# Expert rounds: the bias added by TensorE in every chunk, and the transposes of gathered rows placed behind the activation's

## The reference

```python
def expert_block(args):
    x_i, e = args                                # rows of one expert's tokens
    gu = x_i @ w_gate_up[e] + b_gate_up[e]       # 1024 x 2048, and the bias
    gate, up = jnp.split(gu, 2, axis=-1)
    gate = jnp.minimum(gate, SWIGLU_LIMIT)
    up = jnp.clip(up, -SWIGLU_LIMIT, SWIGLU_LIMIT)
    act = (up + 1.0) * (gate * jax.nn.sigmoid(SWIGLU_ALPHA * gate))
    return act @ w_down[e] + b_down[e]           # 1024 x 1024
```

## Time and profile before

| | us |
|---|---|
| median of 3 runs | 2780.39 (2773.59 to 2784.25) |
| the profiled execution | 2776.94 |
| its span | 2775.3 |
| TensorE busy (PE) | 2586.3, 93% |
| TensorE loading weights (PEld) | 2093.9, 75% |
| VectorE (DVE) | 1993.8, 72% |
| ScalarE (ACT) | 1633.8, 59% |
| GpSimd (POOL) | 401.8, 14% |

### The profile page before, as it was taken

How to read it: one execution, slowest core, us unless ns; L and a number is a source line. 1 busy time by engine, 2 the same in 40 slices (tenths; PEclk the granted TensorE clock), 3 DMA queues, 4 the chain that set the end, 5 groups by cost and what they waited for, 6 DMA issues and landing times.

```text
span 2775.3 us, 41771 instructions
## 1 busy us (share of the span) xinstructions
PE 2586.3 (93%) x12297; PEld 2093.9 (75%) x12297; DVE 1993.8 (72%) x2832; ACT 1633.8 (59%) x2352; POOL 401.8 (14%) x518
## 2 busy tenths in 40 slices
PE   4999899996798948999999999999999999999998
PEld 3888667775687737777777888888888888888886
DVE  5333044453655677676767999999999999999998
ACT  5122144343342326565656888888888888888885
POOL 0000010101000231111111211111111112111110
PEclk7999999997799969999999999999999999999999
DMA  6652222211344347767666999999999999999997
GB/s 235 250 193 103 71 88 79 86 50 49 108 139 159 128 162 280 248 236 252 237 232 237 392 372 378 381 378 376 372 378 377 374 376 385 375 371 375 380 377 270
DMA packets 156570, 715.45 MB, mean 258 GB/s; under 512 B 23180, under 2 KB 43582, under 8 KB 91860
## 3 DMA queue, kind: packets, MB, share of 16 engines
q1 hardware_dynamic: 129680, 641.61, 60.0%
q0 software_dynamic: 26752, 72.92, 9.8%
q10 hardware_dynamic: 68, 0.02, 0.0%
HBM read 659.48 MB, written 64.60 MB: 261 GB/s over the span
## 4 chain that ended last, share of the span: by engine, by line
PE 58%; issue 2%; DVE 2%; ACT 1%; ACTq 0%; DVEq 0%
PE e_pgu L90 11%; PE e_pgu L89 11%; PE e_pgu L88 11%; PE e_pdn L88 6%; PE e_pdn L90 5%; PE e_pdn L89 5%; PE e_pat L2411 2%; PE e_pxt L2403 2%; PE e_pgu L2473 1%; PE e_pgu L2416 1%; PE e_pgu L2417 1%; PE e_pdn L2417 1%; PE e_pdn L2416 1%; ACT e_gu_hi L2090 1%; DVE e_act L2725 0%
## 5 line engine op out<-in xcount | busy, mean ns | idle before, releaser
L2094 DVE TENSOR_TENSOR e_gu_lo<-gu_raw,e_gu_hi 128x1024 fp32r<-128x1024 f32 x676 | 800.6, 1219 | 71.2 <-ACT e_gu_hi L2090 65.8
L2090 ACT ACTIVATE e_gu_hi<-gu_raw 128x1024 fp32r<-128x1024 f32 x676 | 681.4, 1055 | 14.0 <-PE e_pgu L90 11.2
L88 PE MATMUL e_pgu<-e_gu_hi,e_x_hi 128*128 128x512 f32 x1344 | 547.0, 407 | 7.1 <-issue 7.1
L90 PE MATMUL e_pgu<-e_gu_hi,e_x_lo 128*128 128x512 f32 x1344 | 528.0, 393 | 0.0
L89 PE MATMUL e_pgu<-e_gu_lo,e_x_hi 128*128 128x512 f32 x1344 | 526.6, 392 | 0.0
L2699 DVE TENSOR_TENSOR e_dn_lo<-dn_raw,e_dn_hi 128x1024 fp32r<-128x1024 f32 x336 | 398.3, 1220 | 9.7 <-ACT e_dn_hi L2516 9.0
L2516 ACT ACTIVATE e_dn_hi<-dn_raw 128x1024 fp32r<-128x1024 f32 x336 | 345.1, 1059 | 5.2 <-PE e_pdn L2417 2.8
L90 PEld LDWEIGHTS e_pgu<-e_gu_hi,e_x_lo 128*128 128x128 f32 x1344 | 252.9, 188 | 54.6
L88 PEld LDWEIGHTS e_pgu<-e_gu_hi,e_x_hi 128*128 128x128 f32 x1344 | 254.0, 189 | 46.3 <-issue 7.5
L89 PEld LDWEIGHTS e_pgu<-e_gu_lo,e_x_hi 128*128 128x128 f32 x1344 | 254.0, 189 | 39.7
L88 PE MATMUL e_pdn<-e_dn_hi,e_a_hi 128*128 128x512 f32 x672 | 266.5, 397 | 5.9 <-DVE e_a_lo L2742 5.9
(11 more groups left out here) (480 smaller groups left out, 4501.5 us busy)
## 6 DMA issues: line engine op xcount, KB each, us to landing
gu_raw<-in_w_gate_up_dram SPq DMA_DIRECT2D x336, 1024.0 KB
dn_raw<-in_w_down_dram SPq DMA_DIRECT2D x168, 1024.0 KB
wada_later<-in_w_ada_dram SPq DMA_DIRECT2D x32, 512.0 KB, 3.7
win_raw<-in_w_in_dram POOLq DMA_DIRECT2D x5, 2048.0 KB
proj_by_token<-out_stage SPq DMA_DIRECT2D x32, 256.0 KB, 2.0
wg_raw<-in_w_in_dram POOLq DMA_DIRECT2D x16, 512.0 KB, 4.5
gates_transposed<-g_stage POOLq DMA_DIRECT2D x32, 256.0 KB
gate_in<-gates_transposed SPq DMA_DIRECT2D x16, 512.0 KB
```

The source lines that it names most:

```text
L88: pe.matmul(out, a[0], w[0], start=first, stop=False)
L90: return pe.matmul(out, a[1], w[0], start=False, stop=last)
L2090: act.activation(m.gu_hi[:, b, 2 * j:2 * j + 2], m.gu_raw[:, b, 2 * j:2 * j + 2].rearrange("p k g n -> p k (g n)"), ACT.Copy).then_inc(m.g ...
L2094: dve.tensor_tensor(m.gu_lo[:, b, 2 * j:2 * j + 2], m.gu_raw[:, b, 2 * j:2 * j + 2].rearrange("p k g n -> p k (g n)"), m.gu_hi[:, b, 2 * j ...
```

## The change

- TensorE adds the bias in every unit: `by_pe` is gone, and with it `with_biases` on VectorE, the branch of `swish` that reads its result, the loads of bias rows with SyncE's wait ahead of them, and the store of bias rows in the routing phase. The rows of final_g, which shared that buffer, get one of their own and no wait. The clamp of `up` is always made from PSUM, behind the wait for `swish`.
- The transposes of gathered rows stand directly behind `turn_a`. In rounds of two: group 0 in (2, slot 1), 1 in (2, slot 0), 2 in (3, slot 1), 3 in (3, slot 0). In rounds of one: group 2 in chunk 2, group 3 in chunk 3. Only a first round of one keeps two groups behind the down product.
- On ScalarE the general list (rounds of two) moves `stage_x` with them, behind `high_a`. In `single` only the arguments of `swish` change.
- At the end of a round of two's last unit, `swish` comes before the second `high_x`, and `activate` before the second `low_x`.

```diff
@@ TensorE, in the loop over k
                         if k == (TURN_A_K if l else 3) and (l or not first):
                             turn_a(n - 1)
-                        if k == FIRST_K and s == 0 and c >= 2 and ahead:
-                            turn_x(r + 1, 2 * c - 3)
+                            if c >= 2 and (s == 0 or two):
+                                turn_x(r + 1, 2 * c - (4 if s else 3) if ahead else c)
...
-                        if k == KT // 2 and by_pe(two, c, s):
+                        if k == KT // 2:
...
-                            if (c, s) == (CH - 1, 1 if two else 0):
+                            if (c, s) == (CH - 1, 0):
                                 ins.then_inc(pick_used, 1)
...
@@ TensorE, behind the down product
-                    if s == 0 and c in (1, 2):
-                        turn_x(r + 1, 2 * c - 2 if ahead else c + 1)
+                    if first and not two and c in (1, 2):
+                        turn_x(r + 1, 2 * c - 2)
@@ ScalarE, swish
-            def swish(n, parity, on_pe, s=0):
+            def swish(n, parity, s=0):
...
-                elif on_pe:
+                else:
                     act.wait_ge(hidden, n + 3)
                     act.wait_ge(activated, n + 1)
                     act.activation(sg[:], p_gu[:, parity, 0], ACT.Gelu_apprx_sigmoid).then_inc(swished, 1)
-                else:
-                    act.wait_ge(with_bias, n + 3)
-                    act.activation(sg[:], gb[:, 0], ACT.Gelu_apprx_sigmoid).then_inc(swished, 1)
@@ ScalarE, rounds of one: stage_x stays where it is
                     if c:
-                        swish(n - 1, (c - 1) % 2, True)
+                        swish(n - 1, (c - 1) % 2)
@@ ScalarE, rounds of two
                         high_a(n - 1, ps if l else 0)
+                    if s == 1 and c >= 2:
+                        if c == 2:
+
+                            act.wait_ge(x1_lo_done, r + 1)
+                        stage_x(r + 1, 2 * c - 4)
                     if s == 0 and c >= 2:
                         stage_x(r + 1, 2 * c - 3)
...
-                        act.wait_ge(hidden, n + 3)
+                        swish(n, l % 2)
                         high_x(r + 1, 1)
-                        swish(n, l % 2, by_pe(two, c, s))
...
-                    if s == 0 and c in (1, 2):
+                    if not two and c in (1, 2):
@@ SyncE
-                    if two and c < CH - 1:
-
-                        wait_apart(sp, with_bias, U + 2 * c + 2)
-                        bs(here, c + 1, (c + 1) % 2)
@@ VectorE
-                    elif l and not by_pe(two, pc, ps):
-                        with_biases(n - 1, pc, (l - 1) % 2, r)
```

More of the change, by code:

```diff
@@ L43 @@
 FC = FF // CH
-FIRST_K = 6
 TURN_A_K = 5
@@ L1928, in _ @@
                 load_dn(m, sp, 0, c, c, m.dn_in[c])
[L1929 to L1932, removed]
         @block.gpsimd
@@ L2107, in phase_experts @@
     with ExitStack() as ctx:
-        gu_raw, dn_raw, bias, pick = m.gu_raw, m.dn_raw, m.gu_bias, m.pick
+        gu_raw, dn_raw, pick = m.gu_raw, m.dn_raw, m.pick
         gu_hi, gu_lo = m.gu_hi, m.gu_lo
@@ L2132, in phase_experts @@
         gu_in, dn_in, gathered, rows_in = m.gu_in, m.dn_in, m.gathered, m.rows_in
-        bias_in = [sem(f"e_bias_in{i}") for i in range(2)]
         gu_hi_done, gu_lo_done = m.gu_hi_done, m.gu_lo_done
@@ L2197, in units @@
                 yield l, c, s, s == 0, seq[l - 1]
-        def by_pe(two, c, s):
-            return not two or c == 0 or s == 1
         def kept(eng, value):
@@ L2612, in single @@
                 act.wait_ge(hidden, swish_last + 3)
-                swish(swish_last, (CH - 1) % 2, True)
+                swish(swish_last, (CH - 1) % 2)
                 high_x(r + 1, 1)
@@ L2650, in body @@
                     if l:
-                        swish(n - 1, (l - 1) % 2, by_pe(two, pc, ps), ps)
+                        swish(n - 1, (l - 1) % 2, ps)
                         if ps:
@@ L2699, in dn_piece @@
                 dve.tensor_tensor(dn_lo[:, b, j], dn_raw[:, b, j], dn_hi[:, b, j].bitcast(F32), ALU.subtract).then_inc(dn_lo_done, 1)
[L2701 to L2706, removed]
             def with_low(n, parity):
@@ L2720, in activate @@
                     return
-                if on_pe:
-                    dve.tensor_scalar(gb[:, 1], p_gu[:, parity, 1], 1.0 - LIMIT, 1.0 + LIMIT, ALU.max, ALU.min).then_inc(up_clamped, 1)
-                    dve.sem_inc(with_bias, 1)
+                dve.tensor_scalar(gb[:, 1], p_gu[:, parity, 1], 1.0 - LIMIT, 1.0 + LIMIT, ALU.max, ALU.min).then_inc(up_clamped, 1)
+                dve.sem_inc(with_bias, 1)
                 dve.wait_ge(up_clamped, n + 3)
@@ L2793, in body @@
                         with_low(n - 1, (l - 1) % 2)
-                    elif l and not by_pe(two, pc, ps):
-                        with_biases(n - 1, pc, (l - 1) % 2, r)
                     piece()
                     if l:
-                        activate(n - 1, (l - 1) % 2, by_pe(two, pc, ps), ps)
+                        activate(n - 1, (l - 1) % 2, ps)
                         piece()
@@ L2805, in body @@
                         low_x(r + 1, 0)
-                        if not by_pe(two, c, s):
-                            with_biases(n, c, l % 2, r)
+                        activate(n, l % 2)
                         low_x(r + 1, 1)
-                        activate(n, l % 2, by_pe(two, c, s))
                     while todo:
@@ L2838, in combine_tiles @@
     k.bd = over("c_bias_rows", [3 * NE, D], F32, dn0)[:]
-    k.gf = over("c_final_g", [P, D], F32, m.gu_bias_at)[:]
+    k.gf = m.final_g_rows[:]
     k.bd3 = over("c_bias_parts", [3 * NE, D], F32R, dn0 + 4 * D)[:]
```

25 lines of the change are left out of this document (4 added, 21 removed).

## The result

The changed kernel is slower: 2928.76 us (median of 5 runs, 2908.14 to 2937.55) against 2778.59 us (5 runs), a ratio of 1.0539 with a 95% interval of 1.0505 to 1.0573. The forecast was 2892 us with a range of 2866 to 2927: right in its sign and in the place and the mechanism of the waits, 37 us too low at the median and 2 us outside the range.

A forecast was written before the change was run, and what follows sets the result against it. TensorE was taken to set the time in both kinds of expert rounds. From 2776.9 us, 123 us for rounds of one and −7.6 us for rounds of two gave 2892 us, range 2866 to 2927.

The forecast's parts named there:

- The stall in the rounds of one: Chunks 2 and 3: ScalarE's copy delays high_a and the down product, net 3.62 us a round, 123 us in 34 rounds.
- the clock falls: Rival: each new wait in rounds of one costs 5 us at 1.2 GHz, 170 us more, 3062 us; chance 0.05.
- the 14 waits of 0.7 us: Rounds of two: TensorE's waits for the activation, 10.2 us in all, taken as gained; they had left the clock at 1.00.
- The prediction's own sign of being wrong: TensorE: products standing 0.43 us apart behind the waits would show the prediction wrong.
- Rounds of two: Seven rounds: waits gained 10.2 us, transpose switches saved 2.2, bias products lost 4.8; net −7.6 us.
- Late loads: Rival: SyncE issues two loads behind each late piece later, DMA queues run dry; 31 us more, 2923 us; chance 0.12.
- Hidden: Rival: ScalarE or VectorE makes up the late copy within the unit, only savings stay, 2764 us; chance 0.05.
- only one unit: Rival: in rounds of one only one unit pays, chunk 2 being absorbed, 2826 us; chance 0.04.
- The routing phase and the loads: Routing phase's bias-row stores, 21 bias-row loads and SyncE's wait ahead of gate/up loads: dropping them changes nothing.

The follow-up runs named there:

- e1: Changed kernel with stage_x in ScalarE's list for rounds of one moved from between the down pieces to behind high_a: 2761.88 us, ratio 0.9956.
- e2: Kernel before with only the transposes of rounds of one moved behind turn_a, the copy staying where it was: 2927.89 us, ratio 1.0558.
- e9: Changed kernel with 7 unused products added on TensorE in chunk 3's wait in rounds of one, none in chunk 2: 2885.90 us, ratio 1.0395.
- e6: Changed kernel with chunk 3's group of transposes in rounds of one back behind the down product of chunk 2: 2821.24 us, ratio 1.0166.
- e7: Changed kernel with all transposes and copies at their old places, TensorE still adding the bias in every chunk: 2785.86 us, ratio 1.0043.
- e13: Changed kernel with 14 unused products added behind the down product of chunk 1 in rounds of one, where nothing hides them: 2945.14 us, ratio 1.0615.
- e3: Changed kernel with unused products added in TensorE's waits in rounds of one, 10 in chunk 2 and 14 in chunk 3: 2885.12 us, ratio 1.04.
- e8: Kernel before with only the transposes and copies of rounds of two moved as in the change, VectorE adding the bias: 2763.42 us, ratio 0.9958.
- e12: Kernel before with all groups of transposes moved and the copy behind high_a in both ScalarE lists, bias as before: 2760.86 us, ratio 0.9937.
- e4: Changed kernel with only the transposes of rounds of one back behind the down products of chunks 1 and 2: 2764.18 us, ratio 0.9958.
- e5: Changed kernel with chunk 2's group of transposes in rounds of one back behind the down product of chunk 1: 2832.65 us, ratio 1.0216.
- e14: Changed kernel with chunk 2's group in rounds of one back behind chunk 1's down product, plus 14 unused products there: 2938.74 us, ratio 1.0589.

## Why the prediction was right and wrong

- *The stall in the rounds of one* (forecast 3.62 us a round, 123 in all): measured 3.55 and 121. Right, its place too: e1 and e2 show that it is all and only the copy's place in `single`, once the transposes are moved. Within it, chunk 2's unit was off by 0.03 us and chunk 3's by 0.14, where `low_x` takes 0.60 us from start to start and not 0.71.
- *The clock*: this is the step that failed. The text gave "the clock falls" a chance of 0.05 and left it out of the sum and of the range, on the strength above all of one row: a wait of 2.75 us behind which the clock was 1.00. That row shows that a wait of that length needn't lower the clock, not that it doesn't, and the 14 waits of 0.7 us, its other ground, are shorter than the 1.0 us that did nothing in e9. In e2, e6, e7, e9 and e13 the clock fell at that very wait, and in the changed kernel at shorter ones. Sized by the runs, the term is 24 us in the profiled execution and some 44 us at the median (e3), on a sum of 115. The prediction's own sign of being wrong, products 0.43 us apart behind the waits, came true. The rival as I put it, 5 us at the lower level behind every wait, was wrong as well: a fall is 3.4 us long, costs 1.6, and comes behind chunk 3's wait alone (the first round's longer one apart), in 15 to 30 of the 34 rounds of the profiled executions with both that wait and a round of 39.3 us.
- By the Trainium skill ("TensorE: Matmul & The Clock Gate", "A second HAM failure mode: psum-queue depth-cycling") the clock swings where TensorE idles often between groups of matmuls. The changed kernel agrees, with 15 falls against none before, and the prediction was wrong to set this aside; but e13, with the same waits, has three, so how often TensorE idles doesn't settle it.
- *Rounds of two* (forecast −7.6 us): measured −9.8. The waits went, as forecast. e7 and e8 show that they go with the transposes and the copy and not with the bias; the copy alone wasn't moved in any run. The term that was off is the price of a wait, which costs more than its idle time: the row shows a product as busy for 0.39 us while the next could start after 0.23, so each wait loses 0.16 us more than its bracket says, 2.2 us in 14 waits. Where the groups stand behind the activation's transposes they start 0.21 us behind them (2125.38, 2125.59), where I took 0.14. Even so they save something: a round of one takes 35.65 us in e1 and e12 and not 35.75, 0.05 a group where I had 0.08, and the seven rounds of two of e8 are 14.2 us shorter than before (421.1), of which 12.4 are the waits by this reading and 1.8 are left, against my 2.2. The bias cost 4.2 us (forecast 4.8). That makes −10.0 for the measured −9.8.
- *Late loads*: no. From 1530 to 2710 us ScalarE waits for no load in the changed kernel, and the DMA share is 0.90, as forecast for a round that grows.
- *Hidden* and *only one unit*: no, by the 60 waits in 1180 us, two in each round.
- The routing phase and the loads: nothing to be seen of them, as forecast, though 3 us could hide: e4, without the loads and stores, pays 4.2 us for the bias and comes out only 0.8 us above e8, which has them, and the interval of each ratio is some 4 us to either side.

## What to carry to other kernels

When an instruction that signals is moved later on one engine, look in the other engine's list at what stands behind the one that waits for it: here a copy that nobody needed soon held back the one that TensorE needed next, and moving one line behind it turned 5% slower into 0.4% faster. Price waits that are new to a saturated TensorE twice, once as time and once as a risk to its clock, and widen the range by the second; one wait in a trace that left the clock alone is no evidence that sixty-eight will. If such a wait can't be removed, work put into it that nobody needs can be faster than idling.

## What the runs showed of the hardware

- The clock falls with TensorE already busy again, 1.5 us after a wait of 1.84 us has ended (1.3 to 1.5 behind nearly every fall in rounds of one; 0.7 in one of e13's), stays at the lower level for 3.4 us, and costs 1.6.
- Whether it falls depends on the wait and on when it comes. Adding 1.64 us of work to each round took the falls from 2 to 30 in one kernel (e5 to e14) and from 15 to 3 in another (the changed kernel to e13).
- A fall lengthens its round from 39.3 to 40.96 us, and in e14 every round from the fifth on is that long and has one. That one fall brings on the next is a guess that no run tests; the length alone doesn't do it, as e13's undisturbed rounds of 41.0 us show. The number of falls also differs between executions of the same kernel, which is why the changed kernel's runs spread over 29 us. Those of e3, with hardly a difference in clock, spread over 9.
